# Mixture-of-experts passes: token rows turned by VectorE instead of TensorE, and expert matrices loaded in quarters of 512 KB

## What is computed

```python
D_MODEL = 1024; SEQ = 1024; DEPTH = 2
N_GROUPS = 4; EXP_PER_GROUP = 8; N_EXPERTS = 32; TOP_K = 2; D_EXPERT = 512

def run_block(args):
    tok, e = args
    xb = x_pad[tok]
    return (jax.nn.silu(xb @ w1[e]) * (xb @ w3[e])) @ w2[e]
...
y = yb.reshape(P, D) * slot_g[:, None]
return jax.ops.segment_sum(y, slot_t, num_segments=T + 1)[:T]
```

## Time and profile before

| | |
|---|---|
| median of 3 runs | 2504.75 us (2503.08 to 2508.81) |
| the profiled execution's own time | 2503.7 us |
| its span, first to last instruction | 2501.9 us |
| TensorE busy | 2349.0 us (94%) |
| VectorE busy | 1053.3 us (42%) |
| ScalarE busy | 359.8 us (14%) |
| GpSimd busy | 158.3 us (6%) |
| DMA, mean rate over the span | 229 GB/s |
| mean granted TensorE clock | 0.98 of full |
| expert stage, layer 0 | 855 to 1407 us of the span |
| expert stage, layer 1 | 1905 to 2453 us of the span |

### The profile page before, as it was taken

How to read it: one execution, slowest core, us unless ns; L and a number is a source line. 1 busy time by engine, 2 the same in 40 slices (tenths; PEclk the granted TensorE clock), 3 DMA queues, 4 the chain that set the end, 5 groups by cost and what they waited for, 6 DMA issues and landing times. The chain is left out here.

```text
span 2501.9 us, 32697 instructions
## 1 busy us (share of the span) xinstructions
PE 2349.0 (94%) x14145; PEld 1036.5 (41%) x14146; DVE 1053.3 (42%) x2071; ACT 359.8 (14%) x645; POOL 158.3 (6%) x179
## 2 busy tenths in 40 slices
PE   4999999989999899999999799999998999999992
PEld 3555444554555533333333444444554333333331
DVE  1788377757845422222212353444453222221215
ACT  2210333331012200000000230000221000000002
POOL 2000000001000000000000000000000000000000
PEclk9999999999999999999999899999999999999996
DMA  9577110020130599999999521113107999999976
GB/s 316 189 267 258 34 26 26 24 104 34 68 151 34 220 347 408 401 401 411 396 403 402 197 85 51 51 34 118 42 34 273 389 402 402 409 400 411 402 308 253
DMA packets 137739, 574.18 MB, mean 229 GB/s; under 512 B 14783, under 2 KB 39591, under 8 KB 86008
## 3 DMA queue, kind: packets, MB, share of 16 engines
q1 hardware_dynamic: 119496, 526.48, 54.5%
q0 software_dynamic: 18016, 45.31, 4.8%
q10 hardware_dynamic: 80, 0.26, 0.0%
HBM read 550.74 MB, written 38.03 MB: 235 GB/s over the span
## 5 line engine op out<-in xcount | busy, mean ns | idle before, releaser
L1665 PE MATMUL ps<-arena 128*32 128x512 f32 x6144 | 680.0, 595 | 9.1 <-DMA arena<-in_ex_w_dram 8.9
L1665 PEld LDWEIGHTS ps<-arena 128*32 128x32 f32 x6144 | 192.0, 110 | 428.1 <-issue 428.1
L1691 PE MATMUL ps<-arena 128*32 128x512 f32 x3072 | 338.5, 592 | 0.0
L2382 DVE TENSOR_SCALAR arena<-ps,gain_x,mod 128x128 f32<-128x128 f32 x376 | 124.4, 404 | 347.3 <-PE ps L1650 347.3
L1794 PE MATMUL ps<-arena 128*128 128x512 f32 x616 | 264.5, 592 | 0.0
L1542 PE MATMUL ps<-arena 128*128 128x512 f32 x512 | 229.4, 598 | 1.6 <-DVE arena L2194 1.6
L1691 PEld LDWEIGHTS ps<-arena 128*32 128x32 f32 x3072 | 101.3, 110 | 227.6 <-issue 227.6
L2414 DVE TENSOR_TENSOR arena<-ps,gates 128x512 f32<-128x512 f32 x96 | 61.9, 686 | 287.7 <-PE ps L1691 287.7
L1794 PEld LDWEIGHTS ps<-arena 128*128 128x128 f32 x616 | 117.0, 190 | 147.3 <-issue 147.3
L1355 PE MATMUL ps<-arena 128*128 128x512 f32 x384 | 167.3, 593 | 0.7 <-issue 0.7
L2390 DVE TENSOR_TENSOR arena<-arena,ps 128x512 f32<-128x512 f32 x48 | 53.1, 1107 | 242.1 <-PE ps L1665 242.1
(11 more groups left out here) (304 smaller groups left out, 2111.8 us busy)
## 6 DMA issues: line engine op xcount, KB each, us to landing
arena<-in_ex_w_dram SPq DMA_DIRECT2D x384, 1024.0 KB, 9.9
arena<-in_mod_w_dram SPq DMA_DIRECT2D x24, 2048.0 KB, 8.8
arena<-expert_rows SPq DMA_DIRECT2D x16, 1024.0 KB, 8.2
arena<-in_od_w_in_dram SPq DMA_DIRECT2D x12, 1024.0 KB, 5.3
arena<-in_x_dram SPq DMA_DIRECT2D x2, 4096.0 KB, 14.7
normed_rows<-arena POOLq DMA_DIRECT2D x16, 512.0 KB, 2.9
arena<-in_ev_w_in_dram SPq DMA_DIRECT2D x3, 2048.0 KB, 13.1
arena<-in_ev_w_in_dram SPq DMA_DIRECT2D x12, 512.0 KB, 4.1
```

Source lines behind the costliest of these rows:

```text
L1665: ins = nc.tensor.matmul(bank(2 + m)[c:c + n], x[:, j, c:c + n], w_slot(e % 2, m, KC, FE)[:, j], start=j == 0, stop=j == KC - 1)
L1691: ins = nc.tensor.matmul(bank(5 + half)[c:c + n], HT[:, j * P + c:j * P + c + n], w_slot(e % 2, 2, FC, D)[:, j, half * 512:(half + 1) * 51 ...
L2382: ins = V.tensor_scalar(XT[:, b, j * P:(j + 1) * P], bank(j // 4)[:, (j % 4) * P:(j % 4 + 1) * P], gain_x[:, 2 * l + 1, j:j + 1], mod[:, l ...
```

## The change

TensorE no longer turns the token rows, except those of the first pass of a layer. They are gathered in four pieces of 256 elements per slot (four indirect DMAs, from a view of `normed_rows` with four pieces to a row, so that one 32-slot group's pieces lie where the turn needs them). VectorE turns 32x32 blocks in four instructions from `XG` to `XT`, then applies gain and shift in place. ScalarE writes the normed rows with their columns in another order. The indices of the pieces (`PIECE`) come from the table of slots by 16 small matmuls and a few VectorE instructions. The first pass is gathered as before, and turned by 32 matmuls against the identity.

The matrices come in quarters of 512 KB, each issued once its own quarter of the product is done (`part_mm`, three counts in a product, then the product's own semaphore). At the start of the stage, one more matrix of expert 0 is issued ahead of the waits for `lg_mm`, `hn_out` and `x_full[0]`.

```diff
+        row_pieces = rows_hn.rearrange("s (g f) -> (s g) f", g=4)
...
+        def parts_before(l, p):
+            return 9 * NP * l + max(9 * p - 3, 0)
...
-                def weights(e, m, halves=(0, 1)):
-
-                    for half in halves:
+                def weights(e, m, quarters=(0, 1, 2, 3)):
+
+                    for q in quarters:
                         if m == 2:
-                            js = slice(half * 2, half * 2 + 2)
-                            dst = w_slot(e % 2, m, FC, D)[:, js]
...
+                            dst = w_slot(e % 2, m, FC, D)[:, q:q + 1]
...
                 weights(0, 0)
                 weights(1, 0)
+                weights(0, 2 if l else 1)
                 sp.wait_ge(lg_mm, TT * (l + 1))
                 sp.wait_ge(hn_out[0], 16 * (TT // 2) * (l + 1))
                 sp.wait_ge(hn_out[1], 16 * (TT // 2) * (l + 1))
-                sp.wait_ge(x_full[0], 16 * (l * NP // 2 + 1))
-                weights(0, 2 if l else 1)
+                sp.wait_ge(x_full[0], gathered(l, 0))
                 weights(1, 1)
...
                         for m, mm in ((0, up_mm), (1, gate_mm)):
-                            sp.wait_ge(half_mm, halves_before(l, p) + m + 1)
-                            for e in freed:
-                                weights(e, m, (0,))
+                            for q in range(3):
+                                sp.wait_ge(part_mm, parts_before(l, p) + 3 * m + q + 1)
+                                for e in freed:
+                                    weights(e, m, (q,))
                             sp.wait_ge(mm, n0 + p + 1)
                             for e in freed:
-                                weights(e, m, (1,))
+                                weights(e, m, (3,))
...
+                for t in range(4):
+                    pool.indirect_dma_start(
+                        XG[:, b, t * 256:(t + 1) * 256], None, row_pieces,
+                        bass.IndirectOffsetOnAxis(ap=PIECE[:, t * NP + p:t * NP + p + 1], axis=0),
+                        bounds_check=4 * SEQ - 1, oob_is_err=False).then_inc(x_full[b], 16)
...
                     pass_up(p, 0).then_inc(up_mm, 1)
-                    if p + 1 < NP:
-                        turn(p + 1)
                     pass_up(p, 1).then_inc(gate_mm, 1)
...
                 def x_cols(p):
-                    dve.wait_ge(x_T, 2 * (n0 + p + 1) - (p == 0))
-                    columns_of_x(l, p % 2, xt_ready, True, KC if p else KC // 2)
+                    b = p % 2
+                    dve.wait_ge(x_full[b], gathered(l, p))
+                    for t in range(4):
+                        ins = V.transpose(XT[:, b].rearrange("p (j t) -> p j t", j=KC)[:, :, 32 * t:32 * t + 32],
+                                          XG[:, b, t * 256:(t + 1) * 256].rearrange("p (j r) -> p j r", j=KC))
+                    ins.then_inc(x_T, 1)
+                    dve.wait_ge(x_T, n0 + p + 1)
+                    if p == 1:
+                        dve.wait_ge(xt_ready, 2 * (n0 + 1))
+                    for j in range(KC):
+                        x = XT[:, b, j * P:(j + 1) * P]
+                        ins = V.tensor_scalar(x, x, gain_x[:, 2 * l + 1, j:j + 1], mod[:, l, 3, j:j + 1],
+                                              ALU.mult, ALU.add)
+                        if j % 4 == 3:
+                            ins.then_inc(xt_ready, 1)
```

More of the change, by code:

```diff
@@ L803, in experts @@
                     pool.wait_ge(hn_out[b], 16 * (TT // 2) * (l + 1))
-                pool.wait_ge(row_ready, l + 1)
-                for p in range(4):
+                pool.wait_ge(row_ready, 2 * l + 1)
+                gather(l, 0)
+                pool.wait_ge(row_ready, 2 * l + 2)
+                for p in range(1, 4):
                     gather(l, p)
@@ L1610, in mix_and_route @@
                 table_of_rows(TT - 1)
-                spare(11, 2)
+                spare(3, 2)
+                pe.wait_ge(hot_ready, t0 + l + TT + 1)
+                for t in range(4):
+                    for g in range(4):
+                        ins = nc.tensor.matmul(bank(7)[32 * g:32 * g + 32, (4 + t) * NP:(5 + t) * NP],
+                                               ident[:, 32 * t:32 * t + 32], TOK_F, start=True, stop=True)
+                ins.then_inc(tab_mm, 1)
+                spare(8, 2)
             pe.wait_ge(hmix_ready, 2 * HC)
@@ L1693, in pass_down @@
                                                        start=j == 0, stop=j == FC - 1)
-                        if j == 1:
-                            ins.then_inc(half_mm, 1)
+                        if j < FC - 1:
+                            ins.then_inc(part_mm, 1)
                     ins.then_inc(y_mm, 1)
-                turn(0)
+                pe.wait_ge(x_full[0], gathered(l, 0))
+                for j in range(KC):
+                    for g in range(4):
+                        ins = nc.tensor.matmul(
+                            bank(j // 4)[32 * g:32 * g + 32, (j % 4) * P:(j % 4 + 1) * P],
+                            XG[:, 0, g * 256 + j * 32:g * 256 + j * 32 + 32], ident, start=True, stop=True)
+                ins.then_inc(x_T, 1)
                 pe.wait_ge(h_ready, 2 * TT * (l + 1))
@@ L2377, in overflow_tables, with columns_of_x @@
                 dve.sem_inc(ov_tab, 1)
-            def columns_of_x(l, b, done, halves, last=KC):
-                for j in range(last):
+            def columns_of_x(l, b, done):
+                for j in range(KC):
                     ins = V.tensor_scalar(XT[:, b, j * P:(j + 1) * P],
```

94 lines of the change are left out of this document (56 added, 38 removed).

## The result

The changed kernel took 2512.1 us (median of 13 runs, 2502.6 to 2520.6), the kernel before beside it 2506.2 us (13 runs): ratio 1.0025, interval 1.0013 to 1.0036. It is slower by 6 us, where 9 us less were forecast. The profiled execution has a span of 2510.1 us against 2501.9.

A forecast was written before the change was run, and what follows sets the result against it. The prediction held TensorE to set the pace in the expert stages, with DMA transfers barely keeping up and becoming the bound. Middle -4, start -3, end -2 us gave -9 on 2504.75: 2496 us, range 2472 to 2520.

The forecast's parts named there:

- The turn leaves TensorE: Expert stages: 1.16 us a turn, 46 turns, 53.4 us if nothing else were near; three passes take 64.0 us.
- Packets of 4 KB: Weight transfers in the expert stages: quarters halve the packet size, 3% more per byte, 1.8 us a group (1.2 to 3.3).
- Gathers in 1 KB pieces: Token row gathers: half of the rows' share falls from 396 to 325 GB/s, 0.5 us a group.
- Loss of full rate: Middle of the stage: buffers come free in uneven lots, quarters fill some dips; 0.9 us lost a group of three passes.
- Transfers become the bound, and the waits lie at the gate product of the first pass of a group: Middle of the stage: group takes 67.2 us against TensorE's 64.0, waits of 3.2 us a group, only -4 us gained.
- A fixed cost per transfer priced at nothing: Weight transfers: about 2 us fixed cost for each of 8 more a pass lies beside other transfers, so costs nothing.
- VectorE, GpSimd, SyncE: Expert passes: VectorE's four turns take 1.7 to 4.5 us; they, the gathers and 16 transfer issues add nothing to the path.
- Start of the stage: First pass of each layer: gather 2.1 us later, up product 2.7 later, gate product finds its matrices; -3 us (-6 to +4).
- End of the stage: Last down product of both layers: its last piece, now 512 KB, lands 1.2 us sooner; -2 us.
- The clock: Rival, gate products after weight waits: TensorE's clock falls in each of 15 groups, up to +19 us, 2515 us; chance 0.10.
- Slower by packets: Rival, middle of the stage: 4 KB packets at the far bound, a group takes 68.7 us, 2518 us; chance 0.20.

The follow-up runs named there:

- ten spares: The changed kernel with ten spare matmuls between up and gate product in the first pass of every group: 2514.6 us, ratio 1.0023 to the kernel before.
- pieces: The changed kernel with 1 MB transfers, each taking every other 4 KB of a partition's rows, so in 4 KB packets: 2533.2 us, ratio 1.0118.
- halves: The changed kernel with its matrices in transfers of 1 MB (8 KB packets) instead of quarters: 2496.6 us, ratio 0.9958 to the kernel before.
- five spares: The changed kernel with five spare products before the gate product of each group's first pass: 2513.0 us, ratio 1.0026; on another chip 2508.7 us, 1.0006.

## Why the prediction was wrong

Direction and size were wrong, by 15 us (9 less were forecast, 6 more came); the time lies in the range, between the rivals. Step by step:

- **The turn leaves TensorE**: right. 64.0 us a group is TensorE's need; ten spares on top made 68.62.
- **Packets of 4 KB**, 1.8 us a group: right in the rate (411 against 423 GB/s, 2.9%), and in the group: pieces took 1.6 us more than halves on one chip, quarters, with their finer release, 1.0 more on another. Without them the change is faster than the kernel before, so they decide the direction.
- **Gathers in 1 KB pieces**, 0.5 us: too much. The rows' queue moved 10.80 MB in 5165 packets at 7.3%, before 11.13 MB in 4611 at 7.2%: the pieces still went in packets of 4 KB. That is 378 against 394 GB/s per full share, 4%, or 0.2 us a group.
- **Loss of full rate, 0.9 us a group: this is the term that failed.** With the gathers' 0.2 the group needed 66.0 us at full rate and took 68.4: the loss is 2.4 us, where I had 0.9. I counted bytes per group as if they could flow at any time. Since both buffers of a pair come free in the last pass of a group, and are wanted at the gate product of the next pass, a burst of 8.4 MB has 27 us, with the rows and other transfers among it, and slack elsewhere in the group can't be used; the same bytes taken from the gate matrix instead of the down matrix were worth some 27 us more. What part of the 2.4 us is the low clock isn't separated: with five spares, which took most of it away, the groups still took 68.5 us on the mean. My text had the uneven release in it, as a reason for a small number. The twelve whole groups of the middle gave +9.5 us (68.4 against 67.6 on the mean) where I had -3; of the passes around them the second and third, which have no such burst before them, gave 4.6 back, and the last three took 0.8 more. Of the 17 us between the forecast of the span and its measure this is 9.7, the start 3.1, the end 2, and 2.4 lie outside the stages.
- **Transfers become the bound, and the waits lie at the gate product of the first pass of a group**: right, 14 waits, 35.9 us, about 2.6 us each where I said 3.
- **A fixed cost per transfer priced at nothing**: held. Twice the transfers were under way beside each other at a share of 1.00, landing in 9.9 us as before. The prediction's 2 us are what the Trainium skill, "DMA: Bandwidth & Descriptors", in its section on the anatomy of a DMA, states for DMAs that GpSimd issues; the matrices go by SyncE's queue, and no run here shows a fixed part. The Trainium skill, "DMA: Bandwidth & Descriptors", "Rules for kernel authors", asks for 1 MiB or more a transfer; the halves, which keep to it, are faster than the change, but the pieces keep to it too and are slower. What these runs show is the size of a packet, not that of a transfer.
- **VectorE, GpSimd, SyncE**: right. VectorE's turn and columns in the timeline:
```profile
1096.54 1.10 DVE L2418 TENSOR_TENSOR arena<-arena,ps 128x512 f32<-128x512 f32 x1 [9.66 <-PE ps L1677]
1103.41 1.29 DVE L2463 TENSOR_TENSOR arena<-ps,gates 128x512 f32<-128x512 f32 x2 [5.76 <-PE ps L1701]
1104.62 1.41 DVE L2436 STREAM_TRANSPOSE arena<-arena 128x256 f32<-128x256 f32 x4
1106.07 2.14 DVE L2444 TENSOR_SCALAR arena<-arena,gain_x,mod 128x128 f32<-128x128 f32 x8
```
Four turns take 1.41 us (records overlap; 0.40 us each), a little less than my low end of 1.7, and VectorE then stands idle for 9.66 us until its next operation.
- **Start of the stage, -3 us**: measured -0.9 and +1.0. The timeline of layer 0, against the earlier trace rows:
```profile
855.79 3.64 PE L1711 MATMUL ps<-constants,arena 128*32 128x128 f32 x64 [3.65 <-DMA arena<-normed_rows,arena]
859.36 3.48 PE L1208 MATMUL ps<-constants 128*128 128x256 f32 x10
862.78 13.94 PE L1677 MATMUL ps<-arena 128*32 128x512 f32 x128
```
The gather, issued at 848.87, was there 6.9 us later, 2.4 more than before: I had said 2.1. But TensorE waited 3.65 us for it, the clock fell, and the turn took 3.64 us instead of 1.7, the ten spares behind it 3.48 instead of 2.43. So the up product came 6.2 us later where I said 2.7. With halves the gather was there 5.7 us after its issue and the clock stayed up:
```profile
849.94 1.95 PE L1711 MATMUL ps<-constants,arena 128*32 128x128 f32 x64 [1.97 <-DMA arena<-normed_rows,arena]
851.83 2.43 PE L1208 MATMUL ps<-constants 128*128 128x256 f32 x10
```
The gate product had its matrices, as forecast.
- **End of the stage, -2 us**: wrong, nothing. I read the 6 us ahead of the last down product as the landing of its last piece. Between the two products stand 24 records of spare products, 5.35 us, and they do in both kernels (12.79 and 12.75 us from one start to the next). Before, at the place of the earlier trace rows, and with the change:
```profile
1395.23 5.35 PE L1193 MATMUL ps<-constants 128*128 128x256 f32 x24
```
```profile
1390.68 7.05 PE L1701 MATMUL ps<-arena 128*32 128x512 f32 x64
...
1398.15 5.35 PE L1208 MATMUL ps<-constants 128*128 128x256 f32 x24
1403.43 7.07 PE L1701 MATMUL ps<-arena 128*32 128x512 f32 x64
```
- **The clock**, the rival with 0.10: the mechanism is there, and more often than I read from before. I had read that 3.10 us of waiting costs nothing; in the changed kernel waits of 3.15 and 2.34 us were followed by a slow product, and one of 2.90 us was not. With the low clock mostly gone the time fell by 2.4 us, 8 at most, so it isn't the main part of the 15.
- **Slower by packets**, 0.20, had the right sign and 2518 us, with the wrong reason for its size: the packets cost 3%, under its own 3.5%, and the loss of rate was not its 0.9 us.

## What to carry to other kernels

A share of 1.00 of the DMA engines over a whole period doesn't say that the bytes of the period are the bound: find the buffers that come free last and are wanted first, and divide what must land between the two by the full rate. Before cutting a transfer finer, look at the run that it takes from each partition: here, where the transfers are the bound, the change with its transfers kept at 8 KB a partition was 10 us faster than the kernel before, and 13 to 17 faster than with 4 KB. Nor are 8 KB enough: transfers of 64 partitions kept them and were by far the slowest. Before costing a gap ahead of an instruction, look at what fills it: it may be filler that was put there on purpose.

## What was unexpected of the hardware

- A packet of 8 KB took 309 ns, one of 4 KB 160 ns (medians): 2.9% more time per byte in saturated stretches (411 against 423 GB/s).
- Gathers of 1 KB pieces moved as packets of 4 KB and cost 4% more per byte (378 against 394 GB/s per full share of their queue). Four per pass, each of a quarter of the rows, landed in 6.2 us in the median, one of whole rows in 8.7; with the matrices in halves the four took 8.1.
- With weights in transfers of 64 partitions the engines moved 241 GB/s at a share of 1.02, with packets of 8 KB at 567 ns.
- The same kernel had stalls of 0.2 to 0.7 us inside its products on one chip (2513.0 us) and none on another (2508.7 us).
